# One more fp32 product on 64 rows behind the turns of each stage's first chunk, in a two-layer transformer kernel

## The chip, the cores and the metric

The kernel runs on one core of one Trainium2 chip. The metric is the device time of one execution in microseconds. Engines are named as in the profile: PE is TensorE's products, PEld its weight loads, DVE VectorE, ACT ScalarE, POOL GpSimd, SP SyncE.

## What is computed

One sequence of 256 tokens of width 1024 passes two blocks of two layers each, all in fp32. Cut to what matters here:

```python
# first block
for layer in range(2):
    if layer == 0:   # h @ w_in; spatial gating and an RWKV-7 time mix; @ w_out
        ...
    else:            # h @ w_qkv (1024 x 3072); dilated attention; @ w_out
        ...
    x = x + conv_glu_ffn(rmsnorm(x, ff_norm[layer]), w_up, conv_w, conv_b, w_down)   # 1024 x 5632, 2816 x 1024
x = rmsnorm(x, final_norm)
# second block, modulated by mod = silu(c) @ w_ada (1024 x 6144 per layer)
for i in range(2):
    if i == 0:       # qkv, block attention, @ w_o
        ...
    else:            # short convolution: h @ w_in (1024 x 3072), gates, @ w_out
        ...
    x = x + g_f * swiglu(h, w_gate_up[i], w_down[i])                                  # 1024 x 5632, 2816 x 1024
```

Each stage is a norm, a wide product with weights from memory, work between, and a product back to width 1024 that is added to x.

## The kernel before

All of the program is one sequence per engine, written out by hand, with semaphores between the engines. Weights come from memory through a ring of two buffers. ScalarE rounds each half chunk of 128 x 2048 to fp32r (`WHI`, L599) and VectorE writes the rest that rounding left (`WLO`, L605); there are four such pairs of buffers (`NB = 4`), and a pair comes free when TensorE has used it. The activation is held in two such parts too, transposed: `h[0]` (in the profile `ghi`, in the first norm `hhi`) and `h[1]` (`glo`). A product of fp32 accuracy is therefore three products: high times high, high times low, low times high.

Three forms of it make up nearly all of TensorE's work:

- **Tiles** (`pe_tile`, L1044, products on L1060, L1061 and L1062): the weights are stationary (128 columns) and 256 tokens move. One tile is one half chunk: two halves `a` of eight steps over k, three products each, so 48 products into one bank of PSUM. Waits stand only at the tile's start, for the weights and for the bank.
- **Rows** (`pe_rows`, L1075 to L1077, and the first chunk of a stage in `pe_first`, L829 to L831): the activation is stationary and 256 columns of the weights move.
- **Sums** (`pe_sum_part`, L1089): the product back to width 1024, 512 columns move. `pe_ada_sums` (L2610, L2611) has two products of 512 columns for the modulation of the second block.

Seven stages begin with `pe_first`: it multiplies the stage's first chunk while the second half of the norm is still under way, so its result lies with tokens in the partitions. ScalarE copies it to `XN`, and TensorE turns it back with fp32 transpositions against the identity (`pe_turn_back`, L861). In six of the stages these turns stand inside the first full tile, between its half `a = 0` and its half `a = 1`: in the four feed-forwards (`pe_ffn`, norms 1, 3, 5, 7), in the query-key tiles of the dilated attention (norm 2) and in the input tiles of the short convolution (norm 6). The seventh stage, the block attention, calls `pe_turn_back` from its own list. There are eight turns of 128 x 128 in each place.

Behind the six places further tiles follow at once: five in a feed-forward, four in the query-key stage before its scores, nine in the convolution stage. In a feed-forward the order after that comes from `walk`: groups of tiles and of sums by turns, 48 or 96 products of one kind and then of the other.

Some products use only 64 of the array's 128 rows, because their operands lie in 64 partitions: the scores of the dilated attention (L2511, L2513), the small products of the time mix (L2240 and others). These are plain fp32.

`CT` holds constants: an identity at `C_ID` and ones at `C_ONE`, both loaded at the start.

Of the kernel before, what the change touches and what calls it, by code (L numbers as in the profile page):

```python
# [28 lines left out]
C_ID, C_ONE, C_BLK, C_HM = 0, 128, 256, 384  # L29
# [409 lines left out]
def program(nc, A, consts, out):  # L439
    with ExitStack() as ctx:  # L440
        def sb(name, cols, dt=F32, rows=128):
            return ctx.enter_context(nc.sbuf_tensor(name, [rows, cols], dt))
# [31 lines left out]
        CT = sb("consts_sb", NC)  # L474
# [28 lines left out]
        def ht(k):  # L503
            return HT1 if k else HT0
# [15 lines left out]
        def read_out(key):  # L520
            b, n = bank_of[key]
            return bank_sems[b], n + 1
# [7 lines left out]
        def opened(e, key):  # L530
            b, n = bank_of[key]
            if n:
                e.wait_ge(bank_sems[b], n)
            return PS[b]
# [93 lines left out]
        def taken(e, w):  # L628

            i = w.taken  # L630
            w.taken += 1
            e.wait_ge(S["w_lo"], i + 1)
            return WHI[i % NB], WLO[i % NB]
# [219 lines left out]
        def pe_turn_back(e, k, keys):  # L853

            for j, key in enumerate(keys):
                ps = opened(e, key)
                for n in range(2):
                    e.wait_ge(*read_out(("first", k, n)))
                    for a in range(2):
                        c = 256 * j + 128 * a  # L860
                        x = e.transpose(ps[:, 256 * a + 128 * n:256 * a + 128 * n + 128], XN[:, n, c:c + 128], ident)  # L861
                x.then_inc(S["first_turned"], 1)
# [181 lines left out]
        def pe_tile(e, w, key, k_norm, fresh, pair=False, turned=()):  # L1044

            hi, lo = (WHI[0], WLO[0]) if fresh else taken(e, w)
            ps = opened(e, key)
            h = ht(k_norm)
            for a in range(2):
                o = ps[:, 256 * a:256 * a + 256]  # L1050
                for k in range(NK):
                    if fresh and a == 0 and k % 4 == 0:
                        e.wait_ge(S["h_lo"], 3 + k // 4)
                        if k == 0:
                            e.wait_ge(S["w_lo0"], 1)
                        else:
                            taken(e, w)
                    c = (8 * a + k) * 128 if pair else 256 * k + 128 * a
                    wh, wl = hi[:, c:c + 128], lo[:, c:c + 128]
                    e.matmul(o, wh, h[0][:, k, :], start=k == 0, stop=False)  # L1060
                    e.matmul(o, wh, h[1][:, k, :], start=False, stop=False)  # L1061
                    x = e.matmul(o, wl, h[0][:, k, :], start=False, stop=k == NK - 1)  # L1062
                if a == 0 and turned:
                    pe_turn_back(e, k_norm, turned)
            x.then_inc(S["w_used"], 1)

        def pe_rows(e, w, key, k_norm, q):
# [1155 lines left out]
        def tensor_program(e):  # L2223
# [3 lines left out]
            pe_norm(e, 0)  # L2227
            pe_column(e, 0)
            pe_tile(e, w, ("lora", 0), 0, True)
            pe_tile(e, w, ("k", 0), 0, False)  # L2230
            pe_tile(e, w, ("k", 1), 0, False)
            e.wait_ge(S["lora_in"], 48)
            e.wait_ge(S["lora_tanh"], 1)
# [439 lines left out]
```

## Time and profile before

| | |
|---|---|
| time, median of 3 runs | 1269.74 us (1269.67, 1269.74, 1272.99) |
| the profiled execution | 1273.4 us |
| its span, first to last instruction | 1271.6 us |
| PE busy | 1235.3 us, 97% |
| PEld busy | 1151.5 us, 91% |
| DVE busy | 945.4 us, 74% |
| ACT busy | 718.9 us, 57% |
| mean granted TensorE clock | 0.998 |
| tiles (L1060 to L1062) | 5232 products |
| sums (L1089) | 1440 products |

All rows below are of the profiled execution. Matmuls are pipelined and their ends are modelled, so the duration of one product (280 ns in a tile) is longer than the step from one start to the next; the pace is read from starts. Rows of the timeline merge neighbours of one line: the start is that of the first, the length reaches to the end of the last.

### The profile page before, as it was taken

The page shows a single profiled execution, that of the slowest core. Times are in us where ns is not written, and L with a number is a line of the kernel's source. Part 1 is how long each engine was busy: PE and PEld are TensorE (multiplying, and loading weights), DVE is VectorE, ACT ScalarE, POOL GpSimd, SP SyncE. Part 2 cuts the span into 40 slices and gives each one's busy share as a digit, 9 for nine tenths or more (in the row PEclk, how much of TensorE's full clock was granted, in tenths as well). Part 3 has the DMA queues.
Part 4 walks back from the last instruction along what each step waited for, and adds up shares of the span by engine and source line. Part 5 has one row for each costly group of instructions (what it writes and reads, how often), then busy time and mean ns, then how long its engine had stood idle before and what let it go on. Part 6 is the DMA issues. An engine that isn't in the chain of part 4 may idle for free.

```text
span 1271.6 us, 23514 instructions
## 1 busy us (share of the span) xinstructions
PE 1235.3 (97%) x9891; PEld 1151.5 (91%) x9891; DVE 945.4 (74%) x1279; ACT 718.9 (57%) x1048; POOL 16.5 (1%) x28
## 2 busy tenths in 40 slices
PE   6999999999999999999998998999999999999998
PEld 6999889999899879999988997999998998999997
DVE  5877379888768767999976566799986676677453
ACT  6833477656664667666656555644455644644432
POOL 0012000000000000000000000000000000000000
PEclk9999999999999999999999999999999999999999
DMA  9450287776657156789662534699975356575540
GB/s 322 161 199 4 68 264 234 264 240 205 219 199 265 68 173 224 238 274 311 238 239 79 195 134 134 233 357 338 343 277 207 134 199 199 201 263 199 199 166 34
DMA packets 163875, 263.78 MB, mean 207 GB/s; under 512 B 5869, under 2 KB 98233, under 8 KB 163770
## 3 DMA queue, kind: packets, MB, share of 16 engines
q1 hardware_dynamic: 160586, 259.54, 59.6%
q10 hardware_dynamic: 3184, 2.73, 0.7%
q8 instruction: 79, 1.29, 0.4%
q14 instruction: 26, 0.21, 0.0%
HBM read 261.17 MB, written 1.05 MB: 206 GB/s over the span
## 4 chain that ended last, share of the span: by engine, by line
PE 89%; DVE 5%; ACT 3%; issue 2%; DMA 1%; SPq 0%; ACTq 0%; DVEq 0%
PE ps L1089 24%; PE ps L1060 15%; PE ps L1061 15%; PE ps L1062 15%; PE ps L2334 2%; PE ps L830 2%; PE ps L831 2%; PE ps L829 2%; PE ps L1075 2%; PE ps L1077 1%; PE ps L1076 1%; DVE wlo L605 1%; ACT whi L599 1%; PE ps L809 1%; DMA arena<-in_w_ada_dram 1%
## 5 line engine op out<-in xcount | busy, mean ns | idle before, releaser
L605 DVE TENSOR_TENSOR wlo<-ring,whi 128x2048 fp32r<-128x2048 f32 x194 | 443.2, 2288 | 107.4 <-ACT whi L599 107.4
L1060 PE MATMUL ps<-ghi,whi 128*128 128x256 f32 x1600 | 448.2, 280 | 1.3 <-DVE wlo L605 1.3
L1061 PE MATMUL ps<-glo,whi 128*128 128x256 f32 x1600 | 447.1, 279 | 0.0
L1062 PE MATMUL ps<-ghi,wlo 128*128 128x256 f32 x1600 | 446.5, 279 | 0.0
L599 ACT ACTIVATE whi<-ring 128x2048 fp32r<-128x2048 f32 x194 | 370.6, 1914 | 85.0 <-PE ps L1089 47.6
L1060 PEld LDWEIGHTS ps<-ghi,whi 128*128 128x128 f32 x1600 | 300.5, 188 | 2.8 <-DVE wlo L605 1.5
L1061 PEld LDWEIGHTS ps<-glo,whi 128*128 128x128 f32 x1600 | 299.9, 187 | 1.2
L1062 PEld LDWEIGHTS ps<-ghi,wlo 128*128 128x128 f32 x1600 | 300.1, 188 | 0.0
L1089 PE MATMUL ps<-whi,yhi 128*128 128x512 f32 x480 | 158.6, 395 | 3.0 <-DVE ylo L1985 1.3
L1089 PE MATMUL ps<-wlo,yhi 128*128 128x512 f32 x480 | 156.1, 390 | 0.0
L1089 PE MATMUL ps<-whi,ylo 128*128 128x512 f32 x480 | 155.9, 390 | 0.0
L2155 DVE SCALAR_TENSOR_TENSOR acc<-arena,small,acc 128x512 f32<-128x512 f32 x168 | 126.2, 751 | 6.8 <-DMA arena<-in_w_ada_dram 1.7
L1089 PEld LDWEIGHTS ps<-whi,yhi 128*128 128x128 f32 x480 | 88.5, 188 | 22.3 <-issue 2.7
L1089 PEld LDWEIGHTS ps<-whi,ylo 128*128 128x128 f32 x480 | 90.1, 188 | 19.3
L1089 PEld LDWEIGHTS ps<-wlo,yhi 128*128 128x128 f32 x480 | 90.1, 188 | 18.9
L2194 DVE SCALAR_TENSOR_TENSOR arena<-arena,cols 128x254 f32<-128x254 f32 (+1 forms) x176 | 73.8, 478 | 13.6 <-ACT arena L1709 13.1
L2209 DVE TENSOR_TENSOR ylo<-arena,yhi 128x256 fp32r<-128x256 f32 x88 | 37.1, 421 | 48.3 <-ACT yhi L1726 48.2
L829 PE MATMUL ps<-whi,ghi 128*128 128x256 f32 x224 | 63.7, 284 | 4.4 <-DVE glo L973 4.4
L831 PE MATMUL ps<-whi,glo 128*128 128x256 f32 x224 | 62.8, 280 | 0.0
L830 PE MATMUL ps<-wlo,ghi 128*128 128x256 f32 x224 | 62.8, 280 | 0.0
L1707 ACT ACTIVATE arena<-ps 128x512 f32<-128x512 f32 x44 | 26.3, 598 | 57.0 <-PE ps L1062 55.3
L1713 ACT ACTIVATE arena<-ps 128x256 f32<-128x256 f32 x44 | 16.7, 380 | 73.4 <-PE ps L1062 73.2
(306 smaller groups left out, 1578.5 us busy)
## 6 DMA issues: line engine op xcount, KB each, us to landing
arena<-in_w_ada_dram SPq DMA_DIRECT2D x48, 1024.0 KB, 6.1
ring<-in_ff_w_up_dram SPq DMA_DIRECT2D x44, 1024.0 KB, 7.7
ring<-in_w_gate_up_dram SPq DMA_DIRECT2D x44, 1024.0 KB, 7.2
ring<-in_ff_w_down_dram SPq DMA_DIRECT2D x10, 2048.0 KB, 7.9
ring<-in_w_down_dram SPq DMA_DIRECT2D x10, 2048.0 KB, 8.7
ring<-in_od_w_qkv_dram SPq DMA_DIRECT2D x6, 2048.0 KB, 8.4
ring<-in_w_qkv_dram SPq DMA_DIRECT2D x6, 2048.0 KB, 8.1
ring<-in_w_in_dram SPq DMA_DIRECT2D x6, 2048.0 KB, 7.9
```

Source lines behind the costliest of these rows:

```text
L599: e.activation(shaped(WHI[i % NB], k), v, ACT.Copy).then_inc(S["w_hi"], 1)
L605: e.tensor_tensor(shaped(WLO[i % NB], k), v, shaped(WHI[i % NB], k).bitcast(F32), ALU.subtract).then_inc(S["w_lo"], 1)
L829: e.matmul(o, h[0][:, c, t], wh, start=c == 0, stop=False)
L830: e.matmul(o, h[0][:, c, t], wl, start=False, stop=False)
L831: x = e.matmul(o, h[1][:, c, t], wh, start=False, stop=c == NK - 1)
L1060: e.matmul(o, wh, h[0][:, k, :], start=k == 0, stop=False)
L1061: e.matmul(o, wh, h[1][:, k, :], start=False, stop=False)
L1062: x = e.matmul(o, wl, h[0][:, k, :], start=False, stop=k == NK - 1)
L1089: x = e.matmul(ps[:, :], YT[l][:, src_k + i, t], w[r][:, i, 512 * h:512 * h + 512], start=first, stop=last)
L2155: e.scalar_tensor_tensor(a, AW[:, k, :], SC[:, k:k + 1], a, ALU.mult, ALU.add).then_inc(S["ada_acc"], 1)
L2194: e.scalar_tensor_tensor(t[a][:, lag:256], z[:, 256 * a:256 * a + 256 - lag], conv_col(f, 2 - lag, a * NF + p), t[a][:, lag:256], ALU.mult ...
L2209: e.tensor_tensor(YT[1][:, p % 8, :], tg[r], YT[0][:, p % 8, :].bitcast(F32), ALU.subtract).then_inc(S["y_lo"], 1)
```

## The change

Behind the turns in `pe_tile` one product is added. It multiplies 64 rows of the identity with 64 rows of the ones, in fp32, 128 stationary and 128 moving columns, and writes columns 256 to 383 of the tile's own bank. That is where the tile's half `a = 1` begins; its first product has `start=True` and overwrites it. Nothing reads the added result, it waits for nothing and signals nothing. The condition `a == 0 and turned` holds in the six places named above, once each.

```diff
@@ -1062,6 +1062,7 @@
                     x = e.matmul(o, wl, h[0][:, k, :], start=False, stop=k == NK - 1)
                 if a == 0 and turned:
                     pe_turn_back(e, k_norm, turned)
+                    e.matmul(ps[:, 256:384], CT[0:64, C_ID:C_ID + 128], CT[0:64, C_ONE:C_ONE + 128], start=True, stop=True)
             x.then_inc(S["w_used"], 1)
```

On TensorE, at the first feed-forward, the last turns and the beginning of the half `a = 1` stood so before (`xn` is the copied first result, `consts_sb` the table `CT`, `whi` and `wlo` the weights, `ghi` and `glo` the activation):

```order
L861 MATMUL ps<-consts_sb,xn 128x128 [waits s_bank2,s_bank0]
L861 MATMUL ps<-consts_sb,xn 128x128
L861 MATMUL ps<-consts_sb,xn 128x128 [waits s_bank1]
L861 MATMUL ps<-consts_sb,xn 128x128
L1060 MATMUL ps<-ghi,whi 128x256
L1061 MATMUL ps<-glo,whi 128x256
```

and so now:

```order
L861 MATMUL ps<-consts_sb,xn 128x128 [waits s_bank2,s_bank0]
L861 MATMUL ps<-consts_sb,xn 128x128
L861 MATMUL ps<-consts_sb,xn 128x128 [waits s_bank1]
L861 MATMUL ps<-consts_sb,xn 128x128
L1065 MATMUL ps<-consts_sb 128x128
L1060 MATMUL ps<-ghi,whi 128x256
L1061 MATMUL ps<-glo,whi 128x256
```

Nothing else moves on this engine, and nothing on the others.

## Rows read from the trace of the kernel before

**Rows 1.** The page: TensorE's busy time, and the chain that ended last.

```profile
PE 1235.3 (97%) x9891; PEld 1151.5 (91%) x9891; DVE 945.4 (74%) x1279; ACT 718.9 (57%) x1048; POOL 16.5 (1%) x28
...
PE 89%; DVE 5%; ACT 3%; issue 2%; DMA 1%; SPq 0%; ACTq 0%; DVEq 0%
```

**Rows 2.** By window: length; PE, PEld, DVE, ACT, POOL busy (x count); clock; DMA, GB/s.

```profile
185.85:217.03 31.18, 31.18 (x268) 31.18 (x266) 30.77 (x50) 24.96 (x39) 0.00 (x0) 1.00 0.74 246
...
1001.54:1055.33 53.79, 53.79 (x460) 53.79 (x458) 38.86 (x37) 27.40 (x26) 0.00 (x0) 1.00 0.61 216
```

**Rows 3.** Timeline of VectorE, its weight splits: start us, length us, engine, line.

```profile
204.31 2.29 DVE L605 TENSOR_TENSOR wlo<-ring,whi 128x2048 fp32r<-128x2048 f32 x1
...
215.99 2.29 DVE L605 TENSOR_TENSOR wlo<-ring,whi 128x2048 fp32r<-128x2048 f32 x1
```

**Rows 4.** Timeline of TensorE, first feed-forward: turns, first products, end.

```profile
185.06 1.04 PE L861 MATMUL ps<-consts_sb,xn 128*128 128x128 f32 x8
185.85 0.36 PE L1060 MATMUL ps<-ghi,whi 128*128 128x256 f32 x1
186.06 0.28 PE L1061 MATMUL ps<-glo,whi 128*128 128x256 f32 x1
...
217.03 0.39 PE L1089 MATMUL ps<-whi,yhi 128*128 128x512 f32 x1
```

**Rows 5.** L1060 alone by window, products and weight loads (x count), three stretches.

```profile
186.20:217.02 30.82, 24.29 (x88) 16.33 (x87) 1.00 0.73 244
375.43:400.77 25.34, 19.83 (x72) 13.32 (x71) 1.00 0.80 292
...
1001.89:1055.32 53.43, 42.14 (x152) 28.36 (x151) 1.00 0.61 215
```

**Rows 6.** Timeline of TensorE, two tiles of the first norm, start and end.

```profile
51.90 0.28 PE L1060 MATMUL ps<-hhi,whi 128*128 128x256 f32 x1
...
62.78 0.27 PE L2266 MATMUL ps<-consts_sb,xn 128*128 128x128 f32 x1
```

**Rows 7.** Timeline of TensorE, rows behind products on 64 rows (L2240).

```profile
36.03 1.03 PE L2240 MATMUL ps<-pre 64*128 64x256 f32 x8
36.99 0.38 PE L1075 MATMUL ps<-whi,hhi 128*128 128x256 f32 x1
...
37.45 0.28 PE L1075 MATMUL ps<-whi,hhi 128*128 128x256 f32 x1
...
42.56 0.32 PE L783 MATMUL ps<-consts_sb,pre 88*128 88x88 f32 x2
```

**Rows 8.** Timeline of TensorE: turns, 64 rows (L2511, L2513), 128 rows.

```profile
416.69 0.85 PE L2523 MATMUL ps<-consts_sb,arena 128*128 128x128 f32 x6 [1.01 <-DVE arena L1996]
417.47 0.49 PE L2511 MATMUL ps<-arena 64*128 64x128 f32 x4
417.79 0.60 PE L2513 MATMUL ps<-arena 64*128 64x256 f32 x4
418.32 0.38 PE L1075 MATMUL ps<-whi,ghi 128*128 128x256 f32 x1
418.55 0.28 PE L1076 MATMUL ps<-wlo,ghi 128*128 128x256 f32 x1
```

**Rows 9.** Timeline of TensorE, a tile behind an idle gap (in brackets).

```profile
685.32 0.38 PE L1060 MATMUL ps<-ghi,whi 128*128 128x256 f32 x1 [1.33 <-DVE wlo L605]
685.54 0.28 PE L1061 MATMUL ps<-glo,whi 128*128 128x256 f32 x1
...
686.49 0.28 PE L1060 MATMUL ps<-ghi,whi 128*128 128x256 f32 x1
```

**Rows 10.** Timeline of TensorE, a tile behind 64 rows and 512 columns.

```profile
401.46 0.49 PE L2511 MATMUL ps<-arena 64*128 64x128 f32 x4 [0.69 <-ACT arena L1506]
...
402.88 0.28 PE L1060 MATMUL ps<-ghi,whi 128*128 128x256 f32 x1
...
403.60 0.28 PE L1060 MATMUL ps<-ghi,whi 128*128 128x256 f32 x1
```

## The prediction

> **What bounds the kernel now.** I read the page first: TensorE is busy 97% of the span and holds 89% of the chain that ended last [rows 1]. Little is to be had by moving other engines; what counts is the spacing of TensorE's products. Next I read the stretches by window, from the last turn of each of the six places to the end of the tiles behind it [rows 2]. In the two shown TensorE is busy for the whole stretch, at granted clock 1.00 (its upper level, 2.4 GHz), and the other four read the same. VectorE is busy for 30.77 of 31.18 us in the first, the feed-forward, and for 38.86 of 53.79 in the convolution stage. It runs ahead, though: of its weight splits in order, the one started at 204.31 is what TensorE takes at 217.03, and by 215.99 two more were started [rows 3]. So ten microseconds of cover (206.60 to 217.03) lie between the two engines, and one microsecond gained by TensorE meets no wait there.
>
> Then the timeline, product by product. TensorE's mean durations of 280 ns are modelled and overlap, so only start to start tells the pace. Behind the turns of the first feed-forward the second product of the tile starts at 186.06 and the first product of the next kind at 217.03 [rows 4]. The count by window is 88 of L1060 and as many of L1061 and L1062, 264 in all, of which one starts before 186.06 [rows 5]. 30.97 us over 263 steps is **117.8 ns**. The same 256-column fp32r product runs faster elsewhere: from 51.90 to 62.78 us two tiles, 96 products of the same three lines, take 10.88 us, **113.3 ns** each [rows 6]. The granted clock is the same; it is a second rhythm, not a second clock. It held across the boundary of the two tiles with its waits, and ended at a transposition.
>
> What starts the fast rhythm? At 36.99 us the first product behind a group of 64-row fp32 products starts. Its first three steps take 0.46 us, and then 45 steps from 37.45 to 42.56 take 113.6 ns each [rows 7]. At 418.32, again behind 64-row products [rows 8], it goes on in the same way. There are five such entries in the trace (36.99, 409.97, 418.32, 430.48, 438.45) and all five run fast. Behind transpositions of 128 rows, as in [rows 4], every one of the six stages runs slow. That is the case for the change: it puts a 64-row product exactly between the turns and the second half of the tile. Two things speak against it. All five fast entries are of products whose stationary operand is the activation (L1075 to L1077), while the products behind the change hold the weights (L1060 to L1062). And the one entry of that kind behind an idle gap, at 685.32, goes on slow: ten products on, at 686.49, it has made 8 steps of 118 ns since 685.54 [rows 9].
>
> **The change, part by part.** It adds six products and six weight loads on TensorE, no wait, no signal, no DMA. Nothing reads the result; the tile's second half overwrites it with its first product. All of its cost lies on TensorE and so on the path.
>
> - *Change of rows, in.* Transpositions follow each other at 0.11 us (eight from 185.06, the last product behind them at 185.85) [rows 4]. From six transpositions to 64-row products it takes longer: they end at 417.54, the last lasting 0.27, so it starts at 417.27, and the 64-row one follows at 417.47, 0.20 later [rows 8]. Price 0.09.
> - *Its own weights, not loaded ahead.* The first product behind a change of rows takes 0.23 (418.32 to 418.55) against 0.12 for one with its weights ready [rows 8]: 0.11.
> - *Its own columns.* 128 moving columns of fp32 like a transposition: 0.11 [rows 4].
> - *Change of rows, out.* Pairs of 64-row products of 256 columns: four pairs take 0.96 to the next product (36.03 to 36.99) [rows 7], two pairs 0.53 (417.79 to 418.32) [rows 8]. So a pair costs 0.215 and the change 0.10.
> - *The next product's weights,* exposed again: 0.11; and some 0.01 until the rhythm has settled. In exchange the present entry, 0.21 from 185.85 to 186.06 with its weights half exposed [rows 4], loses about 0.03.
>
> The sum is 0.50 us in each stage, 3.0 us in all six. I take it because each piece has its own row of the same kind. The low end is the columns alone, 0.11 each or 0.7 in all, if both changes of rows could hide; the high end adds one more exposed load, 0.61 or 3.7 in all.
>
> The Trainium skill, "TensorEngine Tiling (Array Packing)", Key Properties, says that changing the tiling mode drains the TensorE; the rows above show such a drain at 0.09 to 0.10 us. The page names no after-effect on later full-array products, and by it alone the change would be a cost of 3.0 us; [rows 6] and [rows 7] show a rhythm that it doesn't know.
>
> *The gain.* If the second half of the tile enters fast and stays so until the first product of 512 columns, each step saves 117.8 - 113.3 = 4.4 ns. There are 263 steps in each of the four feed-forwards, 214 behind the query-key tiles (72 of each kind) and 455 in the convolution stage (152 of each kind) [rows 5]. That is 1721 steps, 7.6 us. Less the cost of 3.0 it leaves **4.6 us**: 0.66 net in a feed-forward, 0.45 in the query-key tiles, 1.5 in the convolution stage. TensorE goes into the next work without an idle gap at 217.03 [rows 4], so the time is not given back; only behind the query-key tiles, where TensorE waits for a copy by ScalarE, up to 0.4 may be lost in the softmax chain. Without the fast rhythm nothing is gained at all.
>
> The sum is made against the profiled execution, 1273.4 us (span 1271.6), and gives 1268.8. The median of the runs shown is 1269.74, 3.7 lower; one of them took 1272.99. I take the difference over to the median: **1265.1 us**. About 0.3%, 3.8 us, is what a measurement of this kernel can tell from no change, and the forecast lies just beyond it.
>
> **The rivals.**
>
> 1. *The rhythm doesn't change.* The tile's second half comes out of the drain slow, as the weight-stationary entry at 685.32 did [rows 9]. Then the cost alone is left: +3.0 us, **1272.7**, within 0.3%. For it: no entry of these three lines was fast by itself. Against it: [rows 6] shows these lines sustaining the fast rhythm, and five of five entries behind 64 rows were fast. The rule of the Trainium skill quoted above ("TensorEngine Tiling (Array Packing)", Key Properties) would give this case.
> 2. *It changes in some stages.* The two rhythms lie 4 ns apart, so an entry may hang on a few nanoseconds. Three feed-forwards fast and the rest slow gives 3 x -0.66 + 3 x 0.50 = -0.5, **1269.2**; other mixtures lie between 1266 and 1272. Against it: the six places issue the same instructions in the same order, and today all six do the same.
> 3. *The fast rhythm outlasts the 512-column products.* Then another 16 tiles of 48 products in each feed-forward run fast: 3072 x 4.4 ns = 13.6 us more, **1251.5**. Against it: behind the 64-row products at 401.46 two products of 512 columns follow, and the tile after them is slow again [rows 10].
> 4. *The other side: the drain leaves a slower rhythm.* That tile behind 64 rows and 512 columns begins with 0.72 us for six steps, 120 ns [rows 10]. Held through 1721 steps, 2.2 ns over today's, it costs 3.9 on top of 3.0: +6.9, **1276.6**. It decides for "slower" from 0.5 ns per step on (0.5 x 1721 = 0.8, and 3.0 + 0.8 = 3.8). Against it: no long run in the trace holds that pace.
>
> **How the numbers follow.** Forecast 0.50; no change of rhythm 0.23; some stages 0.15; outlasting 0.05; slower rhythm 0.07. The forecast's own spread is about 1 us: the cost's bounds, the query-key stage, and later stages that may enter either rhythm afresh. About three quarters of it lie beyond 3.8 us, which with the outlasting and a little of the mixtures gives faster 0.45. Slower has the fourth rival and the edge of the first, 0.10. The rest, 0.45, is no measurable change. The range takes in the forecast with its spread and the first two rivals, and leaves out the third and the fourth: 1263.5 to 1273.4.
>
> **What the profile after would show.** From the last transposition to the second product of the tile's second half some 0.73 us where it is 0.23 now; behind it, in each of the six stretches, 113.3 ns from start to start until the first 512-column product: 29.8 us instead of 30.97 in a feed-forward, 51.6 instead of 53.6 in the convolution stage. If the steps read 118 the first rival holds, if they differ by stage the second, and if tiles behind 512-column products also read 113 the third. The prediction is wrong in its cost if the crossing takes other than 0.6 to 0.85 us.

## The result and the profile after

The change costs time: the median is 1274.34 us (12 runs, 1272.40 to 1276.18) against 1270.93 us (12 runs, 1269.16 to 1272.99) for the kernel before on the same chip. The ratio is 1.0026, with a 95% interval of 1.0018 to 1.0035. The forecast was 1265.1; the first rival, 1272.7 or 3.0 us more than before, is what happened, at 3.4 us more.

The profiled execution took 1273.82 us, its span is 1272.0. TensorE's busy time and the chain read as in [rows 1], with 12 more instructions:

```profile
PE 1235.7 (97%) x9903; PEld 1150.3 (90%) x9903; DVE 945.3 (74%) x1279; ACT 719.4 (57%) x1048; POOL 17.2 (1%) x28
...
PE 89%; DVE 5%; ACT 3%; issue 2%; DMA 1%; SPq 0%; ACTq 0%; DVEq 0%
```

Twelve, not six: 9903 - 9891. The change has six products. All instructions that touch a tile of PSUM, by line; these are the two rows of the added line, after name and count the duration's minimum, median and maximum in ns:

```profile
L1065 PEld LDWEIGHTS ps<-consts_sb x12: 182/184/186, 183.0 to 1096.3; 64*128 64x128 f32 x12
L1065 PE MATMUL ps<-consts_sb x12: 272/322/373, 183.0 to 1096.4; 64*128 64x128 f32 x12
```

One plain fp32 product runs as two passes, each with a weight load of its own. That answers to nothing in the prediction. The timeline of TensorE at the first feed-forward, against [rows 4]:

```profile
182.06 1.04 PE L861 MATMUL ps<-consts_sb,xn 128*128 128x128 f32 x8
183.03 0.49 PE L1065 MATMUL ps<-consts_sb 64*128 64x128 f32 x2
183.44 0.39 PE L1060 MATMUL ps<-ghi,whi 128*128 128x256 f32 x1
183.67 0.28 PE L1061 MATMUL ps<-glo,whi 128*128 128x256 f32 x1
...
214.65 0.62 PE L1090 MATMUL ps<-whi,yhi 128*128 128x512 f32 x2
```

(L1090 is L1089 of before, one line further down.) The last of the eight turns starts at 182.83, as the trace of starts has it. From it to the second tile product at 183.67 are 0.845 us, in four steps of 202, 214, 201 and 228 ns: to the first pass, to the second pass, to the first tile product, to the second. Before, the same crossing took 232 ns (28 and 204). All six places read 0.845 within 1 ns, so a place costs **0.61 us**, 3.68 in all.

Behind the crossing nothing has changed: from 183.67 to 214.65 are 30.98 us for 263 steps, **117.8 ns**, at granted clock 1.00 (the upper of its two levels, 2.4 GHz). By window, all engines, with the columns of [rows 2], and then L1060 alone as in [rows 5]:

```profile
183.03:214.51 31.48, 31.48 (x266) 31.36 (x266) 30.59 (x50) 24.89 (x39) 0.00 (x0) 1.00 0.72 239
```

```profile
183.55:214.50 30.95, 24.48 (x88) 16.43 (x88) 1.00 0.71 236
```

VectorE is as busy as in [rows 2], and TensorE has no idle gap ahead of 214.65, so nothing new waits. The other five stretches (215, 263, 263, 455 and 263 steps) read 118 too. Six of six entries are slow, and the whole cost is left.

**Where the 3.4 us sit.** From the first turn of one place to the first turn of the next (the block attention's turns counted too, and the last stretch to the end of the span), the seven stretches grew by 0.61, 0.32, 0.60, 0.00, 0.65, 0.61 and 0.61 us, 3.40 in all; the 0.00 is the stretch behind the block attention's turns, where nothing was added. From the first turn to the end of the span it is 1271.6 - 185.06 = 1086.5 before and 1272.0 - 182.06 = 1089.9 after, the same 3.4. The query-key stretch with its 0.32 is made of three parts: 0.61 of crossing, 0.19 lost at an unaltered entry that ran slow this time (the chunk of rows at 428.23, behind the kernel's own 64-row products; 430.48 in before), and 0.48 given back in one wait, which was 1.01 in [rows 8]:

```profile
414.45 0.85 PE L2524 MATMUL ps<-consts_sb,arena 128*128 128x128 f32 x6 [0.53 <-DVE arena L1997]
```

**Why the spans look alike.** 1271.6 and 1272.0 seem to say that little happened. But the stretch ahead of the first turn, in which no instruction differs, took 3.0 us less after (185.06 against 182.06). Three things make it up. The first 1.1 are there by the first chunk of rows (36.99 against 35.89): the profile of before kept the slow pace of the start, some 213 ns a product, for longer. By window there (columns of [rows 2]), first of the kernel before, then of the changed one; the granted clock is given as 1.00 in both, although one made 11 products where the other made 19:

```profile
18.80:20.90 2.10, 2.10 (x11) 2.10 (x11) 2.10 (x2) 1.56 (x1) 0.00 (x0) 1.00 1.02 410
...
18.80:20.90 2.10, 2.10 (x19) 2.10 (x19) 2.10 (x2) 1.43 (x1) 0.00 (x0) 1.00 1.03 417
```

The second is a fall of the clock, first in the kernel before:

```profile
68.50:72.00 3.50, 3.50 (x17) 1.88 (x15) 3.50 (x6) 0.60 (x1) 0.00 (x0) 1.00 0.91 369
...
72.00:75.50 3.50, 3.50 (x16) 3.34 (x16) 3.17 (x5) 1.23 (x2) 0.00 (x0) 0.52 0.23 42
```

and of the changed kernel:

```profile
68.50:72.00 3.50, 3.50 (x21) 2.21 (x19) 3.50 (x6) 0.60 (x1) 0.00 (x0) 1.00 0.88 358
...
72.00:75.50 3.50, 3.50 (x33) 3.50 (x33) 3.50 (x6) 2.41 (x2) 0.00 (x0) 1.00 0.28 48
```

In the profile of before the granted clock stood at 0.52 (about the lower level, 1.2 GHz) for 3.5 us and TensorE made 16 products instead of 33. The third is the rhythm of the tiles at 73.88, slow in before and fast after (see the last experiment): 96 steps of 4.4 ns, 0.4 us. By 87.35 (84.25 after) the difference is 3.1; less 1.1 and 0.4, an estimated 1.6 is the fall's. What brings the fall about isn't shown. Just ahead TensorE had made 17 products in 3.5 us in before and 21 after, but the kernel with 256 columns (below) made 20 there and fell to 0.53 in its first profile, and made 16 and stayed at 1.00 in its second. Both kernels have executions of both kinds, as the next profiles show.

### The profile page after: what moved, and what is told of

It reads as the page before. It is cut to its first block, busy times and chain, and to the rows that moved or that the text cites. A ratio compares the mean times of both kernels' runs of the same rounds, so it can differ in the third digit from the quotient of the medians.

```text
span 1272.0 us, 23538 instructions
## 1 busy us (share of the span) xinstructions
PE 1235.7 (97%) x9903; PEld 1150.3 (90%) x9903; DVE 945.3 (74%) x1279; ACT 719.4 (57%) x1048; POOL 17.2 (1%) x28
## 4 chain that ended last, share of the span: by engine, by line
PE 89%; DVE 5%; ACT 3%; issue 2%; DMA 1%; SPq 0%; ACTq 0%; DVEq 0%
PE ps L1090 24%; PE ps L1060 15%; PE ps L1061 15%; PE ps L1062 15%; PE ps L2335 2%; PE ps L830 2%; PE ps L829 2%; PE ps L831 2%; PE ps L1076 2%; PE ps L1078 1%; PE ps L1077 1%; DVE wlo L605 1%; ACT whi L599 1%; PE ps L809 1%; DMA arena<-in_w_ada_dram 1%
## 5 line engine op out<-in xcount | busy, mean ns | idle before, releaser
L1060 PE MATMUL ps<-ghi,whi 128*128 128x256 f32 x1600 | 448.5, 280 | 1.5 <-DVE wlo L605 1.5
L1062 PE MATMUL ps<-ghi,wlo 128*128 128x256 f32 x1600 | 446.6, 279 | 0.0
L1060 PEld LDWEIGHTS ps<-ghi,whi 128*128 128x128 f32 x1600 | 300.4, 188 | 3.7 <-DVE wlo L605 1.7
L1062 PEld LDWEIGHTS ps<-ghi,wlo 128*128 128x128 f32 x1600 | 300.2, 188 | 0.0
L1090 PE MATMUL ps<-whi,yhi 128*128 128x512 f32 x480 | 158.6, 395 | 3.0 <-DVE ylo L1986 1.3
L1090 PE MATMUL ps<-wlo,yhi 128*128 128x512 f32 x480 | 156.1, 390 | 0.0
L1090 PE MATMUL ps<-whi,ylo 128*128 128x512 f32 x480 | 155.9, 390 | 0.0
L1090 PEld LDWEIGHTS ps<-whi,yhi 128*128 128x128 f32 x480 | 88.5, 188 | 22.3 <-issue 2.7
L1090 PEld LDWEIGHTS ps<-whi,ylo 128*128 128x128 f32 x480 | 90.1, 188 | 19.2
L1090 PEld LDWEIGHTS ps<-wlo,yhi 128*128 128x128 f32 x480 | 90.1, 188 | 19.0
L829 PE MATMUL ps<-whi,ghi 128*128 128x256 f32 x224 | 63.6, 284 | 4.5 <-DVE glo L973 4.5
L831 PE MATMUL ps<-whi,glo 128*128 128x256 f32 x224 | 62.7, 280 | 0.0
```

The costliest lines, as they stand in the source:

```text
L829: e.matmul(o, h[0][:, c, t], wh, start=c == 0, stop=False)
L831: x = e.matmul(o, h[1][:, c, t], wh, start=False, stop=c == NK - 1)
L1090: x = e.matmul(ps[:, :], YT[l][:, src_k + i, t], w[r][:, i, 512 * h:512 * h + 512], start=first, stop=last)
```

## The experiments

Twelve more profiles follow. Ten are of kernels that add something else at the same places, or the same thing elsewhere; two are of the two kernels themselves, once more. The altered ones differ from the kernel before only in products that nothing reads. An entry is called fast if its steps behind the second product settle at 113 to 114 ns, slow if at 117 to 118. "Norm 1" and so on are the six places (1, 3, 5, 7 feed-forwards, 2 query-key tiles, 6 convolution).

### Does the length of the added product matter?

```diff
                 if a == 0 and turned:
                     pe_turn_back(e, k_norm, turned)
+                    n = {1: 256, 2: 192, 3: 160, 5: 96, 6: 64, 7: 32}[k_norm]
+                    e.matmul(ps[:, 256:256 + n], CT[0:64, C_ID:C_ID + 128], CT[0:64, C_ONE:C_ONE + n], start=True, stop=True)
```

> The added 64-row product has another number of moving columns in each of the six stages: 256, 192, 160 in the feed-forward of norm 1, the query-key tiles of norm 2 and the feed-forward of norm 3, 96 in the feed-forward of norm 5, 64 in the convolution stage (norm 6), 32 in the last feed-forward (norm 7). Theory A, the pace is chosen by nanoseconds of timing at the entry: since the way out of the product comes at another moment each time, at least one of the six stretches reads 113.3 ns per step and not all agree. Theory B, products with stationary weights can't take up the fast rhythm behind a change of rows: all six read 117.8 ns. Theory C, the 64-row product has to be as long as in the five fast entries (256 columns): only the first stretch reads 113.3. Cost: the product is recorded as two passes, so from the last turn to the second product of the tile's second half it takes 0.61 us over before at 128 columns, and 2 x 0.42 ns per column more or less: 0.72 us at 256, 0.53 at 32 if the second pass waits for its weights (0.107 us).

Measured: 1271.89 us, span 1270.1. With 256 columns at norm 1 the entry was **fast**, and stayed so for all 263 steps:

```profile
182.88 0.70 PE L1066 MATMUL ps<-consts_sb 64*128 64x256 f32 x2
183.51 0.38 PE L1060 MATMUL ps<-ghi,whi 128*128 128x256 f32 x1
183.73 0.28 PE L1061 MATMUL ps<-glo,whi 128*128 128x256 f32 x1
...
183.96 0.28 PE L1060 MATMUL ps<-ghi,whi 128*128 128x256 f32 x1
```

The other five, 192 columns and fewer, were slow. The four steps of the crossing were 202, 320, 306, 222 ns with 256 columns and 202, 133, 202, 222 with 32. Over the six lengths the step between the two passes is 107 ns and 0.83 per column: the second pass's weights are not loaded ahead. In the changed kernel their load starts at 183.14, 107 ns behind the first pass, and the second pass starts 107 ns behind the load. The step out of the second pass grows with the columns likewise from 160 on (226, 252, 306 ns) and is 202 with 96 and fewer. The tiles behind the first products of 512 columns were back at 118 at once.

### Which part costs: rows, form, columns?

```diff
+                    one, c = slice(C_ONE, C_ONE + 128), slice(256, 384)
+                    if k_norm == 1:
+                        for _ in range(2):
+                            e.matmul(ps[:, c], CT[0:64, C_ID:C_ID + 128], CT[0:64, one], start=True, stop=True)
+                    elif k_norm == 2:
+                        e.matmul(ps[:, c], CT[:, C_ID:C_ID + 128], CT[:, one], start=True, stop=True)
+                    elif k_norm == 3:
+                        e.matmul(ps[:, 256:257], CT[:, C_ID:C_ID + 128], CT[:, C_ONE:C_ONE + 1], start=True, stop=True)
+                    elif k_norm == 5:
+                        e.matmul(ps[0:64, c], CT[:, C_ID:C_ID + 64], CT[:, one], start=True, stop=True)
+                    elif k_norm == 6:
+                        e.matmul(ps[0:64, c], CT[0:64, C_ID:C_ID + 64], CT[0:64, one], start=True, stop=True)
+                    else:
+                        e.matmul(ps[:, c], hi[0:64, 0:128], h[0][0:64, 0, 0:128], start=True, stop=True)
```

> Another form of the added product in each stage: two 64-row products (norm 1), one on all 128 rows (norm 2), one on 128 rows with a single moving column (norm 3), 128 rows by 64 columns of the array (norm 5), 64 by 64 (norm 6), and 64 rows in fp32r from the weights and the activation (norm 7). Theory D, cost is two changes of shape plus two passes each with a weight load: over before 0.61 + 0.21 us at norm 1 (a second product adds two passes), about 0.21 to 0.25 at norm 2 and 0.2 or less at norm 3 (no change of shape, weights loaded ahead), 0.61 at norms 5 and 6 (a change of the columns costs what a change of the rows costs), and 0.1 less at norm 7, where fp32r has one pass. A rival, that only a change of rows drains: norm 5 costs no more than norm 2. Rhythm: by theory A some of the six may be fast, and forms with 128 rows as well as the others; by theory B none; if 64 rows do help, only norms 1, 6 and 7.

Measured: 1275.28 us, span 1273.4, clock 0.999; all six slow. At norm 2, the added product on all 128 rows:

```profile
375.57 0.39 PE L1070 MATMUL ps<-consts_sb 128*128 128x128 f32 x2
375.71 0.36 PE L1060 MATMUL ps<-ghi,whi 128*128 128x256 f32 x1
375.92 0.28 PE L1061 MATMUL ps<-glo,whi 128*128 128x256 f32 x1
```

The steps are 109, 112, 31 and 204, in all 456 ns: 0.22 more than without any product, and it is the two passes. At norm 3, with one moving column instead of 128, they are 109, 31, 111 and 205, the same 456: the price is that of two weight loads. At norm 2 the first tile product follows the second pass after 31 ns, as it followed a turn after 28; at norm 3 the 31 lie between the two passes. A second 64-row product behind the first (norm 1) adds 0.22 as well. 64 stationary columns on 128 rows (norm 5) cost the same steps of 203 in and 202 out as a change of rows, so a change of columns drains too. The one fp32r product (norm 7) has one record and three steps, 202, 254, 224: one pass.

### Do 64 rows make every entry fast?

The same product ahead of each half chunk of `pe_rows`, twelve in all, and none behind the turns:

```diff
+                if n == 0:
+                    e.matmul(o[:, 0:128], CT[0:64, C_ID:C_ID + 128], CT[0:64, C_ONE:C_ONE + 128], start=True, stop=True)
```

> The same 64-row product stands ahead of the first product of each of the twelve half chunks with the activation stationary (lines 1075 to 1077), none behind the turns. Before, in the block attention, three of these six run fast (from 699.43, 713.12, 741.90) and three slow (706.34, 719.46, 750.12), and all four of the dilated attention run fast. Theory E, behind 64 rows this form always becomes fast: all of them read 113.3 ns per step, the three slow ones too. Theory A: the mixture changes, and some still are slow. Cost about 0.6 us in each place, less where TensorE waited anyway.

Measured: 1273.43 us, span 1271.6. Eight of the twelve were fast, where nine of twelve are in the kernel before. They were not the same ones: the entries that follow 64-row products of the kernel anyway, all fast before, were slow in two of five places, 407.18 and 435.86. Of the former:

```profile
406.87 0.38 PE L1075 MATMUL ps<-consts_sb 64*128 64x128 f32 x2
407.18 0.39 PE L1077 MATMUL ps<-whi,ghi 128*128 128x256 f32 x1
407.41 0.28 PE L1078 MATMUL ps<-wlo,ghi 128*128 128x256 f32 x1
407.52 0.28 PE L1079 MATMUL ps<-whi,glo 128*128 128x256 f32 x1
...
408.23 0.28 PE L1079 MATMUL ps<-whi,glo 128*128 128x256 f32 x1
```

From 407.52 to 408.23, six steps of 118. This sends the reader back to the trace of before. The prediction had listed the five entries of rows behind 64-row products, all fast, and had not listed the seven others. Here is one of them, behind 128-row products only:

```profile
741.76 0.39 PE L2588 MATMUL ps<-arena 128*128 128x128 f32 x2
741.90 0.37 PE L1075 MATMUL ps<-whi,ghi 128*128 128x256 f32 x1
742.11 0.28 PE L1076 MATMUL ps<-wlo,ghi 128*128 128x256 f32 x1
...
742.45 0.28 PE L1076 MATMUL ps<-wlo,ghi 128*128 128x256 f32 x1
```

It is fast, as are those that start at 46.25, 699.43 and 713.12; those at 706.34, 719.46 and 750.12 are slow. Four of seven without 64 rows ahead were fast: the five of five were a choice of cases.

It doesn't follow that an entry is a toss. In the thirteen profiles in which nothing was added ahead of the rows, 57 of 65 entries behind the kernel's own 64-row products were fast; without 64 rows ahead the chunk at 741.90 (starts as in the kernel before) was fast and those at 706.34 and 750.12 were slow, each thirteen times out of thirteen. In this experiment, with the product ahead, these three came out slow, fast and fast. What stands ahead does shift the odds at a place; one profile of it doesn't tell how much of that is the 64 rows.

### Does the place in the program matter?

The product at the start of every tile behind the first norm that has no turns, 94 entries, and none behind the turns:

```diff
+                if a == 0 and k_norm and not turned:
+                    e.matmul(o[:, 0:128], CT[0:64, C_ID:C_ID + 128], CT[0:64, C_ONE:C_ONE + 128], start=True, stop=True)
```

> The same 64-row product stands at the start of every tile (lines 1060 to 1062) whose norm is 1 or more and which has no turns inside: some 90 entries from three kinds of neighbours, a tile, a sum, a modulation sum. Theory B: no entry is fast, all read 117.8 ns, and the time is 90 x (0.6 to 0.7) = 54 to 63 us over before. Theory A: a part of the entries is fast, and entries with the same neighbours agree with each other.

Measured: 1323.86 us. 81 of the 94 entries were slow; the 13 fast entries are just the 13 that stand directly behind a sum. One of them (L1091 the sum, L1052 the added product, L1062 to L1064 the tile), and one behind another tile:

```profile
228.40 0.39 PE L1091 MATMUL ps<-whi,ylo 128*128 128x512 f32 x1
228.71 0.48 PE L1052 MATMUL ps<-consts_sb 64*128 64x128 f32 x2
229.13 0.38 PE L1062 MATMUL ps<-ghi,whi 128*128 128x256 f32 x1
229.35 0.28 PE L1063 MATMUL ps<-glo,whi 128*128 128x256 f32 x1
...
229.58 0.28 PE L1062 MATMUL ps<-ghi,whi 128*128 128x256 f32 x1
...
205.26 0.49 PE L1052 MATMUL ps<-consts_sb 64*128 64x128 f32 x2
205.68 0.39 PE L1062 MATMUL ps<-ghi,whi 128*128 128x256 f32 x1
205.90 0.28 PE L1063 MATMUL ps<-glo,whi 128*128 128x256 f32 x1
...
206.14 0.28 PE L1062 MATMUL ps<-ghi,whi 128*128 128x256 f32 x1
```

The added product and the crossing out of it are the same instructions in both. In ns the crossings read 318, 213, 202, 222 and then 113 behind a sum, and 209, 213, 202, 225 (in others up to 228) and then 117 behind a tile. The last step of the crossing differs by 3 to 6 ns, and the rhythm goes with it, but for one slow entry in the block attention (757.61) that had 221 as well. This is the only kind of tile entry that was fast in every case, 13 of 13 in this one profile: in the profiles where nothing stands between, the 13 tiles behind a sum are all slow. There is hardly a gain in it. Behind twelve of the 13 sums there are 48 or 96 tile products before one of another kind, worth at most 96 x 4.4 = 0.42 us, and a crossing with the added product costs 0.61 more than one without (0.955 against 0.345); only behind the last sum but one are there 192, worth an estimated 0.85.

### 256 columns at all six places

```diff
-                    e.matmul(ps[:, 256:384], CT[0:64, C_ID:C_ID + 128], CT[0:64, C_ONE:C_ONE + 128], start=True, stop=True)
+                    e.matmul(ps[:, 256:512], CT[0:64, C_ID:C_ID + 128], CT[0:64, C_ONE:C_ONE + 256], start=True, stop=True)
```

> The added product has 256 moving columns instead of 128 in all six stages; in the first feed-forward that form entered the fast rhythm. Theory F, the wide 64-row product sets the fast rhythm at this place whatever the stage: all six stretches read 113.3 ns per step to the first product of 512 columns, gain 1721 x 4.4 ns = 7.6 us; cost by the crossing measured in the first feed-forward (202 + 320 + 306 + 222 = 1050 ns against 232) 0.82 us in each, 4.9 in all; net 2.7 us faster than before, ratio 0.998. Theory A, nanoseconds of timing at the entry: the neighbours are the same in all six, so most agree with the first, but one or two may stay slow, each for 0.82 + 4.4 ns x its steps: between 2.7 us faster and 1 us slower. If the first was chance: all slow, 4.9 us slower.

Measured: 1273.01 us median (12 runs, 1270.29 to 1276.64), ratio 1.0014, interval 1.0002 to 1.0026. In the profile norms 1 and 2 were fast, 3, 5, 6 and 7 slow. Norm 1:

```profile
186.09 0.70 PE L1065 MATMUL ps<-consts_sb 64*128 64x256 f32 x2
186.72 0.38 PE L1060 MATMUL ps<-ghi,whi 128*128 128x256 f32 x1
186.94 0.28 PE L1061 MATMUL ps<-glo,whi 128*128 128x256 f32 x1
...
216.74 0.39 PE L1090 MATMUL ps<-whi,yhi 128*128 128x512 f32 x1
```

29.80 us from 186.94 to 216.74, the figure that the prediction gives for a fast stretch. Its gain of 1.16 against a crossing of 0.82 more than in before makes the stretch 0.35 shorter, as measured.

The same kernel, profiled once more with nothing altered:

> The kernel with 256 columns in all six stages, unaltered, looked at a second time; the first look had two stages fast (norms 1 and 2) and four slow. If the instructions fix the outcome the same two are fast. By theory A the pattern follows the last step ahead of the turns (116 or 117 fast, 121 or 122 slow), and may be another one.

Measured: 1274.67 us, span 1272.9, and all six **slow**. Norm 1 again:

```profile
183.41 0.70 PE L1065 MATMUL ps<-consts_sb 64*128 64x256 f32 x2
184.03 0.39 PE L1060 MATMUL ps<-ghi,whi 128*128 128x256 f32 x1
184.26 0.28 PE L1061 MATMUL ps<-glo,whi 128*128 128x256 f32 x1
...
215.23 0.63 PE L1090 MATMUL ps<-whi,yhi 128*128 128x512 f32 x2
```

30.97 us for the same 263 steps. The crossings were 203, 320, 306, 221 ns in the first profile and 203, 320, 305, 226 in this one. Identical instructions gave both rhythms, and the last step of the crossing tells them apart by 5 ns.

### Other forms, finer lengths, one pass

Five more forms with about 256 columns: norm 1 fp32r on 64 rows, norm 2 fp32 on 128 rows, norms 3 and 5 fp32 on 64 rows with 240 and 224 columns, norm 6 fp32r on 128 rows, norm 7 fp32 on 32 rows.

```diff
+                    if k_norm == 1:
+                        e.matmul(ps[:, 256:512], hi[0:64, 0:128], h[0][0:64, 0, :], start=True, stop=True)
...
+                    elif k_norm == 3:
+                        e.matmul(ps[:, 256:496], CT[0:64, C_ID:C_ID + 128], CT[0:64, C_ONE:C_ONE + 240], start=True, stop=True)
...
+                    elif k_norm == 6:
+                        e.matmul(ps[:, 256:512], hi[:, 0:128], h[0][:, 0, :], start=True, stop=True)
```

> Six forms with 224 to 256 moving columns, one in each stage: fp32r on 64 rows with 256 columns (norm 1), fp32 on 128 rows with 256 (norm 2), fp32 on 64 rows with 240 (norm 3) and 224 (norm 5), fp32r on 128 rows with 256 (norm 6, the plain tile product once more), fp32 on 32 rows with 256 (norm 7). Theory F: fast behind norms 1 and 7 and at 240 columns, slow with 128 rows. Theory A: the form doesn't decide; fast and slow don't sort by rows. Crossings from the last turn to the second tile product, over 232 ns before: norm 1 about 0.5 us (one pass: 202 + 107 + 200 + 222), norm 2 0.43, norm 3 0.79, norm 5 0.76, norm 6 0.12, norm 7 0.82 us.

Measured: 1271.18 us, span 1269.4. Norms 1 and 3 fast, the other four slow. fp32r on 128 rows (norm 6) follows the last turn after 28 ns and is followed by the tile after 204 and 117: one more step of the stream, no drain, 0.12 us.

The lengths 254, 252, 250, 248, 244 and 232 at the six places, in the form of the first experiment:

```diff
+                    n = {1: 254, 2: 252, 3: 250, 5: 248, 6: 244, 7: 232}[k_norm]
```

> The added 64-row product has 254, 252, 250, 248 columns at norms 1, 2, 3, 5, 244 in the convolution stage and 232 at norm 7: two columns less move the way out by 1.7 ns. Theory A: fast and slow change within these few nanoseconds, so the six don't agree and 254 need not do what 256 did. Theory F: from 256 down to some number all are fast, below it all slow, one boundary.

Measured: 1273.3 us, span 1271.5, all six slow. No length near 256 is fast by itself.

fp32r on 64 rows, one pass, at all six:

```diff
+                    e.matmul(ps[:, 256:512], hi[0:64, 0:128], h[0][0:64, 0, :], start=True, stop=True)
```

> The added product is on 64 rows with 256 moving columns, but in fp32r from the tile's own weights and activation, in all six stages. It is one pass: crossing 202 + 313 + 221 ns against 232, cost 0.50 us each, 3.0 in all, and where a stage enters fast it gains 1.17 us (feed-forward), 0.95 or 2.0. Theory A, timing at the entry: the last tile step ahead of the turns tells it. Where it reads 116 or 117 ns the stage goes on fast, where it reads 121 or 122 it goes on slow (ten of ten so far at 240 and 256 columns). With half of the stages fast the time is about that of before, within 1.5 us. Theory F, the wide product does it whatever came before: six fast stages, 4.6 us faster.

Measured: 1270.31 us median (1268.66 to 1274.19), ratio 1.0008, interval 0.9996 to 1.0019: not told from the kernel before. In the profile only norm 1 was fast, with a crossing of three steps, 202, 313 and 221.

Until then a step of 116 or 117 ns ahead of the turns (the last of the tile's first half), rather than 121 or 122, had gone with every fast entry of a wide product, and I had taken it for the cause. Here five of six places had 116 or 117 ahead and four of those were slow. That rule fell. The near-zero cost is no merit of the form either. The crossings cost 0.5 more each, 3.0 in all, and norm 1 gave 1.16 back. Beyond that, the four first chunks (L829 to L831) of norms 3, 5, 6 and 7, which stand *ahead* of the added product and are unaltered, ran fast in this profile where they were slow in before; each is 96 steps, 0.42 us. Another 0.63 is the wait of the query-key stage, 0.38 where [rows 8] has 1.01.

### All 128 rows at all six places

```diff
-                    e.matmul(ps[:, 256:384], CT[0:64, C_ID:C_ID + 128], CT[0:64, C_ONE:C_ONE + 128], start=True, stop=True)
+                    e.matmul(ps[:, 256:384], CT[:, C_ID:C_ID + 128], CT[:, C_ONE:C_ONE + 128], start=True, stop=True)
```

> The added product on all 128 rows instead of 64, at all six places, otherwise as in the change: fp32, 128 columns, the tile's own bank. Theory A (the cost is made of drains, exposed weights and the two passes of an fp32 product; the rhythm of the tiles behind it is picked by the entry's nanoseconds): no change of rows, so both drains and the exposed load go; what is left is two passes of some 0.11 each, 0.22 us at a place as at norm 2 of the kernel of forms, 1.3 us in all. Crossing from the last turn to the second tile product 0.45 us instead of 0.84. Time 1.3 us over the kernel before. Rival (the 64 rows themselves are what costs and what could help): no difference in the crossing beyond 0.2. Rhythm: 117.8 ns in all six, or in single ones 113; with 12 slow entries out of 12 behind 128 columns so far I expect at most one fast.

Measured: 1272.22 us median (11 runs), ratio 1.0017, interval 1.0008 to 1.0026. From the first turn to the end it is 1087.8 us, 1.3 over the kernel before. All six were slow, and all six crossings took 455 or 456 ns (109 or 110, 111 or 112, 30 or 31, 204), as at norm 2 above. So of the change's 0.61 us at a place 0.22 are its two passes and 0.39 the two changes of rows with the weight loads that they expose.

### The two kernels once more, unaltered

The changed kernel:

> The changed kernel unaltered, looked at a second time. If the pace at this place is fixed by the instructions, or if 128 columns leave no entry to the fast rhythm, all six stretches are slow again, with crossings of 845 ns. If theory A holds for 128 columns too, another look may show a fast one.

Measured: 1275.56 us, span 1273.7, with the clock at 0.51 in the window 72.00 to 75.50. All six crossings 840 to 845 ns, all six slow. The kernel before:

> The kernel before, unaltered, profiled once more: what another execution of the same instructions does. Theory A (each entry of a tile takes one of two rhythms by its nanoseconds): the six entries behind the turns read 117.8 ns again, or a single one 113; but entries elsewhere (the tile at 73.88, the rows at 406.98) may read otherwise than in the first profile. Theory B (the rhythm is fixed by the instructions ahead): every entry of the trace reads as in the first profile of the kernel before, to the nanosecond or two. The first segment differs by 2 to 3 us between profiles with the clock fall at 72 to 75.5 us and those without.

Measured: 1270.58 us, span 1268.8, clock at 1.00 in that window with 33 products. The spans of the two kernels at clock 1.00 there are 1268.8 and 1272.0, 3.2 apart; with the fall they are 1271.6 and 1273.7, 2.1 apart. From the first turn to the end the kernel before has 1086.5 and 1086.4 us, the changed one 1089.9 and 1089.1. The 0.8 between the two profiles of the changed kernel lie in unaltered places: 0.4 in the query-key stage, where the entry at 428.23 was fast again and the wait ahead of L2524 fell to 0.3, and 0.4 at the first chunk of norm 5 (796.02) with the tiles behind it, 96 steps that were fast this time.

In the second profile of before the six entries behind the turns are slow again. But entries elsewhere went the other way. The chunk of rows at 719.46 in the first profile:

```profile
719.46 0.47 PE L1075 MATMUL ps<-whi,ghi 128*128 128x256 f32 x1
719.77 0.28 PE L1076 MATMUL ps<-wlo,ghi 128*128 128x256 f32 x1
...
725.30 0.49 PE L2498 MATMUL ps<-consts_sb,arena 128*128 128x128 f32 x3
```

and the same chunk in the second:

```profile
716.82 0.47 PE L1075 MATMUL ps<-whi,ghi 128*128 128x256 f32 x1
717.12 0.28 PE L1076 MATMUL ps<-wlo,ghi 128*128 128x256 f32 x1
...
722.47 0.49 PE L2498 MATMUL ps<-consts_sb,arena 128*128 128x128 f32 x3
```

47 steps in 5.53 us, 117.7 ns, against 47 in 5.35, 113.8 ns. The tiles behind 73.88 and 87.35, slow in the first profile, are fast in the second, as in the changed kernel's; the first chunk at 792.55 is fast where it was slow (795.32). Nothing in the program differs.

## Why the prediction was wrong, point by point

- **The step that failed is the gain**: "If the second half of the tile enters fast and stays so", 1721 steps by 4.4 ns. The rest of that step held wherever an entry of such a stretch was fast (29.80 us for 263 steps). What failed is that 64 rows bring it about. With the change's own product 0 of 12 entries were fast in two profiles, and all 1721 steps stayed at 117.8 ns: 0 us in place of 7.6. With nothing behind the turns it is 0 of 24, in four profiles. Counting all entries behind the turns, 64-row products of at most 192 columns gave 0 of 20, wider ones (224 to 256 columns) 6 of 28, products on 128 or 32 rows 0 of 12. That the wider ones can be fast is shown; that width is the reason isn't, since one and the same kernel gave two of six and then none.
- The reading behind it was "all five run fast". In the same trace four of the seven row entries with no 64 rows ahead were fast as well, and five of five against four of seven doesn't tell the rows' part. The prediction's own doubts, that the five were entries of another form and that the one tile entry in [rows 9] was slow, pointed the right way and were weighed too low.
- **The term that was mis-sized is "its own columns"**, 0.11. A plain fp32 product is two passes, 0.214 apart on 64 rows, each with its own weight load, and the turns, which make one pass, were the wrong row to price it by. The right row was there: [rows 7] has eight records of L2240 where the code issues four products. What the prediction priced at 0.215 as a pair is two records that start 7 ns apart (36.03 and 36.04), it seems one pass on each half of the rows. The price is 0.61 instead of 0.50, the high end of the bounds, though not for their reason (one more exposed load); the crossing is 0.845, at the edge of the 0.6 to 0.85 given.
- The other terms held. The step into the product is 202 ns, as the 0.20 of [rows 8]; out of it 201, as the 0.11 of a pass and the 0.10 for the change of rows, and then 228, as the 0.23 there. The drain of 0.09 to 0.10 each way is in all crossings with a change of rows and in none without (456 ns). The Trainium skill, "TensorEngine Tiling (Array Packing)", Key Properties, says that changing the tiling mode drains the TensorE. These runs agree, for rows and for columns, and the page's rule gave the right sign here.
- **The first rival** was right in mechanism: "then the cost alone is left". It said +3.0 by the same 0.50; with 0.61 it is 3.7. Less the 0.3 net of the query-key stage, that is 3.4. That the medians also differ by 3.4 is in part luck: the other profile of the changed kernel has 2.6 from the first turn to the end, since unaltered entries came out otherwise.
- **The second rival** didn't happen with this product, but its reason, "an entry may hang on a few nanoseconds", is what the runs showed. The prediction argued against it that the six places issue the same instructions and all do the same. Equal instructions turned out to be no warrant.
- **The third and fourth** are excluded. The third needed a fast stretch to be tried on, and the experiments gave some: where the first feed-forward was fast (norm 1 with 256 columns), the tiles behind its first sums were back at 118. It also counts sixteen later tiles in a feed-forward where the trace has fourteen (11.9 us instead of 13.6). As to the fourth, no stretch was slower than 118; its 120 came from six steps read at the entry, and the whole tile of [rows 10] goes at 117.9.
- The cover of VectorE held. In the query-key stage part of the cost was swallowed, as was said for part of a gain, though by another wait: the one on VectorE ahead of L2524 (1.01, then 0.53). The wait on ScalarE's copy stayed at 0.69.
- The base: the profiled execution of before had the slow start and the clock fall at 72.00 to 75.50 and lay 3.7 us above the median shown. Taking the difference over to a median was right; the two profiled spans alone, 0.4 apart, would have hidden the cost. But the median of three runs, 1269.74, was 1.2 below that of twelve, 1270.93. That makes up most of what separates the first rival's 1272.7 from the measured 1274.34.

**What stays open.** What exactly picks the rhythm. The crossing's last step goes with the outcome (221 or 222 wherever a tile behind 64 rows was fast, 224 to 228 in most of the slow entries), but eight slow entries behind the turns had 221 or 222 too, so it is a symptom near the choice and not the choice itself. No run controlled the phase itself, and nothing in the trace shows one. Whether some other spacing makes an entry behind turns reliably fast was not found.

## What to carry to other kernels

Before a pattern in a trace is taken for a cause, list the cases that lack it: the ones with the same outcome and without the supposed cause decide. Take the profile of the same kernel twice before a difference of a few ns per step is put down to an instruction. Price a new product by a row of its own data type and rows, and count the records, since one line of code may be two passes.

## What the runs showed of the hardware that was not expected

- The same stream of 256-column fp32r products with a weight load each runs in one of two rhythms, 113.3 or 117.8 ns, at the same granted clock of 1.00. The slow one was seen to hold for 455 steps, the fast one for 263. The rhythm is mostly set at the entry and may differ between executions of one program. It can also change on the way: in the block attention's first chunk in before (entered at 675.35) the steps are 113 to 114 ns up to 678.05, then 120, 127 and 115, and 117 to 119 to the chunk's end, with no gap between.
- A plain fp32 product takes two passes with a weight load each (214 ns apart with 128 columns on 64 rows, 320 with 256, 133 with 32), an fp32r product one, a transposition one.
- A change of stationary columns from 128 to 64 costs the same drain as a change of rows: 203 in, 202 out. Between products of 128 rows in fp32 and fp32r there is none (31 ns).
- The clock at the start differs between executions of one program. In each kernel one of the two profiles has a longer slow start and a fall of the clock to 0.51 or 0.52 at 72.00 to 75.50. Together with the rhythm of the tiles there they move all that follows: the first turn stands at 185.06 or 182.34 in the kernel before and at 184.64 or 182.06 in the changed one, 2.6 to 2.7 us apart, nearly as much as the change costs. About 1 us of it is there before the fall (the first rows at 36.99 or 35.89, and at 36.81 or 35.89).
